# Banded attention: heads of one score pair on different halves of the array's rows, side by side in TensorE's queue

## The reference, cut to what matters

```python
q = apply_rope(q.reshape(b, s, h, d), cos, sin).reshape(b, nb, BLOCK, kvh, g, d)   # h = 4, kvh = 2, g = 2, d = 64
sc = jnp.einsum('bnqkgd,bnjkd->bnkgqj', q, kb).astype(jnp.float32) * (d ** -0.5)
sc = jnp.where(valid[None, :, None, None], sc, NEG_INF)
sink_l = jnp.broadcast_to(sink.reshape(kvh, g, 1, 1), sc.shape[:-1] + (1,))
p = jax.nn.softmax(jnp.concatenate([sc, sink_l], axis=-1), axis=-1)[..., :-1]
o = jnp.einsum('bnkgqj,bnjkd->bnqkgd', p, vb)
```

## Time and profile before

| what | us |
|---|---|
| median of 3 runs (1536.16 to 1536.81) | 1536.79 |
| the profiled execution's own time | 1534.68 |
| its span, first to last instruction | 1532.8 |
| TensorE busy | 1400.1 (91%) |
| VectorE busy | 488.0 (32%) |
| ScalarE busy | 299.3 (20%) |
| the kernel's mean DMA rate | 301 GB/s |

### The profile page before, as it was taken

One profiled execution on the slowest core, in us unless ns is written; L12 is line 12 of the kernel. 1 busy time (PEld: TensorE's weight loads), 2 busy tenths in 40 slices (PEclk: granted clock), 3 DMA queues, 4 the chain that ended last, 5 costly groups with the idle time before them and its releaser, 6 DMA issues.

```text
span 1532.8 us, 15300 instructions
## 1 busy us (share of the span) xinstructions
PE 1400.1 (91%) x6316; PEld 712.9 (47%) x6316; DVE 488.0 (32%) x891; ACT 299.3 (20%) x515; POOL 126.7 (8%) x100
## 2 busy tenths in 40 slices
PE   6999899999999999989699998999999999999883
PEld 5666568543333333323277564765333333333331
DVE  5764664311101111100459367442111101101105
ACT  2435540100000000000143547111000000000000
POOL 1330001000000000000153100000000000000004
PEclk9999999999999999999989999999999999999997
DMA  9200331999999999999940012448999999999992
GB/s 385 98 1 1 138 139 50 389 363 428 428 426 427 428 427 426 427 428 429 421 189 0 1 55 94 151 196 338 417 428 426 428 428 426 427 427 427 428 427 84
DMA packets 43396, 462.01 MB, mean 301 GB/s; under 512 B 7744, under 2 KB 8384, under 8 KB 14912
## 3 DMA queue, kind: packets, MB, share of 16 engines
q1 hardware_dynamic: 32832, 436.88, 67.9%
q0 software_dynamic: 3744, 13.63, 2.2%
q10 hardware_dynamic: 6752, 10.52, 2.0%
HBM read 450.53 MB, written 10.49 MB: 301 GB/s over the span
## 4 chain that ended last, share of the span: by engine, by line
PE 69%; DMA 16%; DVE 7%; issue 3%; ACT 2%; POOL 1%; SPq 0%; ACTq 0%; POOLq 0%; DVEq 0%
PE bank L865 20%; DMA ring<-w_moe 14%; PE bank L888 12%; PE bank L508 10%; PE bank L839 7%; PE bank L758 2%; PE bank L762 2%; PE bank L761 2%; PE bank L573 1%; PE bank L461 1%; PE bank L827 1%; PE bank L817 1%; PE bank L652 1%; DVE X L1376 1%; PE bank L731 1%
## 5 line engine op out<-in xcount | busy, mean ns | idle before, releaser
L865 PE MATMUL bank<-ring,work 128*64 128x512 f32 x1600 | 354.5, 594 | 19.9 <-issue 10.3
L865 PEld LDWEIGHTS bank<-ring,work 128*64 128x64 f32 x1600 | 128.6, 137 | 221.1 <-issue 189.2
L888 PE MATMUL bank<-ring,w_up 128*64 128x512 f32 x864 | 194.2, 596 | 20.2 <-DMA ring<-w_moe 9.9
L1376 DVE TENSOR_TENSOR X<-X,bank 128x512 f32<-128x512 f32 x128 | 87.9, 687 | 306.0 <-PE bank L839 305.8
L1364 DVE TENSOR_TENSOR work<-work,bank 128x512 f32<-128x512 f32 x32 | 22.0, 687 | 435.8 <-PE bank L865 434.6
L839 PE MATMUL bank<-work,cst 128*128 128x512 f32 x256 | 125.6, 620 | 13.1 <-ACT work L1663 11.2
L888 PEld LDWEIGHTS bank<-ring,w_up 128*64 128x64 f32 x864 | 66.5, 137 | 137.0 <-issue 116.8
L865 PE MATMUL bank<-work 128*64 128x512 f32 x448 | 99.3, 592 | 1.5 <-issue 1.5
L508 PE MATMUL bank<-x_hi,w_hi 128*128 128x512 f32 x288 | 79.7, 421 | 7.7 <-ACT x_hi L1427 6.8
L839 PEld LDWEIGHTS bank<-work,cst 128*128 128x128 f32 x256 | 40.7, 188 | 98.5 <-DVE X L1376 45.0
L1065 DVE SCALAR_TENSOR_TENSOR bank<-X,par,bank 128x512 f32<-128x512 f32 x120 | 80.0, 749 | 0.9 <-DVE ring L1039 0.9
(11 more groups left out here) (205 smaller groups left out, 1537.2 us busy)
## 6 DMA issues: line engine op xcount, KB each, us to landing
ring<-w_moe SPq DMA_DIRECT2D x154, 2048.0 KB, 28.2
work<-w_moe SPq DMA_DIRECT2D x38, 2048.0 KB, 28.6
ring<-w_in SPq DMA_DIRECT2D x18, 1024.0 KB, 22.3
ring<-w_out SPq DMA_DIRECT2D x8, 1024.0 KB, 27.9
out<-X POOLq DMA_DIRECT2D x12, 512.0 KB, 6.1
X<-out ACTq DMA_DIRECT2D x2, 2048.0 KB, 8.4
work<-ln SPq DMA_DIRECT2D x4, 1024.0 KB, 21.8
x_rows<-X ACTq DMA_DIRECT2D x8, 512.0 KB, 3.6
```

Source lines behind the costliest of these rows:

```text
L865: ins = mm(B((kind, pair, n))[64 * e:64 * e + 64, :], xsT[:, k, 64 * e:64 * e + 64], w[:, e, n * 512:(n + 1) * 512], start=(k == 0), stop= ...
L888: ins = mm(B(("O", pair, n))[64 * e:64 * e + 64, :], hidT[:, k, 64 * e:64 * e + 64], w[:, i, e], start=(k == 0), stop=(k == KD - 1))
L1376: nc.vector.tensor_tensor(X[:, t, cols], X[:, t, cols], B(name)[:, :], ALU.add)\
```

## The change: which heads are neighbours, and what stands between them

The array's half becomes `64 * (h % 2)` and the query tile `h // 2`. So head indices 0 and 1 lie on different halves, and so do 2 and 3; index 1 and 2 have swapped meaning, and the sinks are swapped by the host to match. The two heads that `d_values` takes together are now 0 and 2, then 1 and 3. In the loop over blocks, T T S S of heads 0 and 1 stand together, then two fills, then T T S S of heads 2 and 3, a fill, V of the first two, two fills, V, a fill. ScalarE's wait before it overwrites a turned head follows the new pairs.

```diff
-                    rows = slice(64 * (h // 2), 64 * (h // 2) + 64)
+                    rows = slice(64 * (h % 2), 64 * (h % 2) + 64)
                     before(pe, ("SD", i), lay)
-                    mm(B(("SD", i))[:, 0:(hi - lo) * P], gq[rows, h % 2, n * P:(n + 1) * P],
+                    mm(B(("SD", i))[:, 0:(hi - lo) * P], gq[rows, h // 2, n * P:(n + 1) * P],
                        gk[rows, lo * P:hi * P], start=True, stop=True).then_inc(fullsem(("SD", i)), 1)
...
-                        read_out(pe, ("TD", n * GQ_H + 2 * j + e), lay)
+                        read_out(pe, ("TD", n * GQ_H + 2 * e + j), lay)
...
-                            h = 2 * j + e
+                            h = 2 * e + j
...
-                    for h in range(GQ_H):
-                        d_turned(n, h)
-                        d_scores(n + 1, h)
-                        if (n, h) == (2, 3):
-                            for name in (("qup", 0), ("qup", 1), ("kup", 0), ("kup", 1), ("ropeK",), ("ropeQ",)):
-                                read_out(pe, name, lay)
-                            a_scores(0)
-                        else:
-                            fill(6 * n + h)
-                        if h == 2:
-                            if n == 0:
-                                read_out(pe, ("gvT",), lay)
-                            d_values(n, 0)
+                    d_turned(n, 0)
+                    d_turned(n, 1)
+                    d_scores(n + 1, 0)
+                    d_scores(n + 1, 1)
+                    fill(6 * n)
+                    fill(6 * n + 1)
+                    d_turned(n, 2)
+                    d_turned(n, 3)
+                    d_scores(n + 1, 2)
+                    d_scores(n + 1, 3)
+                    fill(6 * n + 2)
+                    if n == 0:
+                        read_out(pe, ("gvT",), lay)
+                    d_values(n, 0)
                     if n < 2:
+                        fill(6 * n + 3)
                         fill(6 * n + 4)
                     else:
+                        for name in (("qup", 0), ("qup", 1), ("kup", 0), ("kup", 1), ("ropeK",), ("ropeQ",)):
+                            read_out(pe, name, lay)
+                        a_scores(0)
                         a_scores(1)
                     d_values(n, 1)
...
-                        if h < 2:
+                        if h % 2 == 0:
                             ac.wait_ge(pvd_done, at(lay, NT, n))
...
-        + [every(a["sink"]), every(a["b_router"])], axis=2)
+        + [every(a["sink"][:, [0, 2, 1, 3]]), every(a["b_router"])], axis=2)
```

## The result

The changed kernel takes 1519.36 us (median of 4 runs, 1517.01 to 1520.51) against 1536.47 us for the kernel before (4 runs, 1532.72 to 1536.81: the three of the table ahead of the prediction and one more): a ratio of 0.9898, 95% interval 0.9885 to 0.991, which is 14 to 18 us less. 1520.6 had been predicted. The profiled execution took 1519.53 us with a span of 1517.7, the one before 1534.68 and 1532.8. The changed kernel is five lines longer behind its loop over blocks, so lines 711, 1117, 1173 and 1509 of before are 716, 1122, 1178 and 1514 in its rows.

What follows compares the result with a forecast made beforehand. TensorE, busy 91% of the span, was taken as the bound; 4.16 + 1.66 + 0.86 + 1.6 - 0.2 = 8.1 us a layer, 16.2 for two, gave a median of 1520.6 us, range 1516.5 to 1530.

Steps and rivals of the forecast that it cites:

- Overlap: Score pairs: two heads on different row halves run wholly at once, a pair for one head's price; chance 0.66.
- half overlap: Rival for the score pairs: three steps instead of two, 11.9 us won, time 1524.9; chance 0.10.
- (a): Blocks 0 and 1, four pairs of 384 columns: second visit, change and load go, 1.04 us each, 4.16 a layer.
- the prediction's signs: Checks named beforehand in the profile, among them blocks 0, 1 and 2 at about 15.6, 16.5 and 13.3 us.
- (b): Block 2, two pairs of 256 columns: 0.83 us saved each, 1.66 a layer.
- (d): Block 2, TensorE's 1.78 us wait for the first dense score on VectorE: 0.2 stays, 1.6 us won a layer.
- (c): Scores of block 0, two neighbouring pairs of 256 columns: only overlap is new, 0.43 us each, 0.86 a layer.
- (e): Block 3: first V waits for one more ScalarE copy (0.38 us), partly covered, costing 0.2 us a layer.
- The sum: All terms in the attention together: 8.1 us won a layer, 16.2 for two layers.
- The margins: Second head's probabilities in time by 0.5 us; in block 1 the fourth score's bank free by 0.3 us.
- the slower case: Rival in blocks 1 and 2: fourth score stalls for a bank VectorE reads late, 19.2 us lost, 1539.8; chance 0.05.
- Given back: Rival after the attention: weight stream not tied to TensorE, experts end as before, about 1536.8 us; chance 0.06.

Runs made afterwards that it cites:

- The last block alone: Kernel before, with the last head's transposes and scores of block 2 ahead of the last fill and first V: 1531.97 us against 1535.85, ratio 0.9979.
- the doubled fills: Changed kernel with 40 projection matmuls done twice in layer 0, the first time for nothing: 1528.66 us against 1535.16 for the kernel before, ratio 0.9961.
- the halves alone: Kernel before with the change's assignment of heads to halves, but the old order of the loop over blocks: 1537.95 us against 1535.85, ratio 1.0018.

## Why the prediction was right, by its steps

**Overlap.** Held in full. The row of line 614, two heads on halves of the columns, was the right neighbour for halves of the rows: the pair costs what one head did. In the sum for that row the prediction took 0.15 us for the visit where it has 0.20 elsewhere; the pairs here fit 0.20 (2 x 0.32 + 0.20 = 0.84, and 2 x 0.215 + 0.20 = 0.63). The half overlap, which the prediction drew from the order of start and end in the Trainium skill (TensorE: Matmul & The Clock Gate, Part 3, The mechanism), is refuted: two of the four instructions start together, and a pair takes two steps, not three. In which order the four stand behind one another no row shows.

**(a) Pairs of 384 columns.** 1.04 us a pair was predicted. Block 1 gives 2.01 for its two (18.54 to 16.53). Block 0 gives 1.20 in place of 2.08, for one reason that the prediction missed: of the two heads that now stand together, the second takes bank 6, and in block 0 the turn before it in that bank is the variance of the convolution group, read by ScalarE (line 1471, 124.30 to 124.99). I had followed the probabilities, the score banks and ScalarE's later chain for the second head, but not the bank that it writes. The second head's transposes start 0.73 us later for it, and with the variance in another bank block 0 is 0.84 us shorter. At 15.66 us it is then within 0.1 of the 15.6 that the prediction's signs had for it. This is the one term of the sum that was mis-sized by more than 0.2 us.

**(b) and (d) Block 2.** 0.83 a pair and 1.6 for the wait make 3.26; measured 3.21. The last block alone gave 1.61 and the rest of the change 1.60 of it, so the two terms are also right one by one, and line 1117 (now 1122) starts 0.2 us behind the fill as was said.

**(c) The pairs ahead of the loop.** 0.86 predicted; 106.87 to 126.64 has become 105.18 to 124.09, 19.77 to 18.91: 0.86.

**(e) Block 3.** 0.2 us was charged for a later copy. It cost nothing: block 3 takes 4.42 us in both (179.39 to 183.81, 170.42 to 174.84). The first V stands behind the last transposes in TensorE's list and starts at 172.84, and ScalarE's third copy ends before that, at 172.64. So the extra copy was covered altogether.

**The sum.** 8.1 predicted for a layer, 7.28 measured. Of the 0.8, block 0 lacks 0.88 (0.84 of it the missed bank), block 1 0.07 and block 2 0.05, and the 0.2 charged for block 3 come back.

**The margins.** The fourth score of block 1 started at 146.76, 6.2 us into the block (6.1 predicted), and VectorE had read the first at 145.84 to 146.32: no wait, with 0.44 us to spare. The first transposes of block 1, at 140.59, found their probabilities: VectorE's divisions for the four heads, 1.41 us in one piece, start at 139.30. So what the slower case needed didn't occur, by less than half a microsecond.

**Given back.** Refuted by the doubled fills: 9.13 us put into the attention came out as about 9 us.

**The median.** 1519.36 against 1520.6: 16.2 us were taken from a median of 1536.8, and 14.6 were really won by the change. The two medians lie 17.1 us apart; the 2.5 us beyond the ledger are not explained by it. That a sum 1.6 us too large gave a time only 1.2 us too high is luck, not accuracy.

## What to carry to other kernels

Two matmuls that contract over 64 rows are worth putting side by side on different halves, with two banks: here a pair took 0.84 us in place of 1.48. Before bringing two instructions together, go through everything the second one needs, its output bank among it, since the work that stood between them was also its cover. And a variant that is slower than the sum of its parts says should first be looked at in its granted clock: the halves alone would have been judged useless by their time.

## What the runs showed of the hardware

Two float32 matmuls on different halves of the rows, writing two banks, ran wholly at once: 0.84 us a pair of 384 columns, against 1.48 on one half. By an estimate from the rows, a visit to the 64-row form costs 0.20 us on top of its instructions, with two or four of them in it and with 256 or 384 columns, and 0.10 more in the group behind it; a V that lost its whole visit saved 0.38. TensorE's clock fell to 1.2 GHz behind an idle time of only 1.78 us that followed some 50 us of work without a wait, in both layers of one kernel's profile, and not in that of another kernel with the same idle time. With two matmuls without a use in that gap the stretch from block 0 to the first dense transpose took 57.11 us in both layers, against 58.81 and 60.46 without them, 5 us in all.
